# A two-block transformer kernel on one core: feature tiles cast one by one as the last projection tile frees them, and weight panels split ahead of the root

## The reference

```
h = rmsnorm(x, gain)                    # x * rsqrt(mean(x*x) + eps) * gain
x = x + mixer(h) @ w_out                # 1024 x 1024: "mix", "pw2", "mix2" in the kernel
h = rmsnorm(x, gain)
x = x + (silu(h @ w_gate) * (h @ w_up)) @ w_down    # 2816 hidden: "up1/dn1", "up2/dn2", "up3/dn3"
```

## Time and profile before

| | us |
|---|---|
| median of 3 runs | 1957.59 |
| lowest and highest run | 1955.42, 1958.98 |
| the profiled execution, its own time | 1949.41 |
| its span, first to last instruction | 1947.6 |
| PE busy | 1857.5 (95%) |
| DVE busy | 1068.3 (55%) |
| ACT busy | 712.2 (37%) |
| POOL busy | 206.7 (11%) |
| mean granted clock of PE | 0.969 |

### The profile page before, as it was taken

The page is one execution under the profiler, slowest core; times in us unless marked ns, Lnnn a source line. Parts: engine busy times, 40 slices in busy tenths (PEclk is TensorE's granted clock), DMA queues, the critical chain, the costliest instruction groups (busy, mean ns, idle before and its releaser), DMA issues.

```text
span 1947.6 us, 22792 instructions
## 1 busy us (share of the span) xinstructions
PE 1857.5 (95%) x8596; PEld 1532.3 (79%) x8596; DVE 1068.3 (55%) x1304; ACT 712.2 (37%) x799; POOL 206.7 (11%) x125
## 2 busy tenths in 40 slices
PE   7899999999999999699999999899999999999997
PEld 5788877888888788477888888678888788888876
DVE  6647654444444678755444433556845544444455
ACT  4326544434333311245343423432223544332343
POOL 1600000000000476300000000011720000000000
PEclk9889999999999999899999999898999999999999
DMA  5310123333233311032333233222113233323332
GB/s 164 102 49 1 44 65 108 87 107 86 81 104 96 87 51 58 22 87 67 106 86 108 73 99 94 81 86 67 53 59 87 76 97 86 108 77 111 89 89 77
DMA packets 280027, 159.49 MB, mean 82 GB/s; under 512 B 7776, under 2 KB 278016, under 8 KB 279968
## 3 DMA queue, kind: packets, MB, share of 16 engines
q1 hardware_dynamic: 278912, 155.44, 27.8%
q0 software_dynamic: 624, 1.67, 0.3%
q10 hardware_dynamic: 432, 1.57, 0.2%
HBM read 156.56 MB, written 2.10 MB: 81 GB/s over the span
## 4 chain that ended last, share of the span: by engine, by line
PE 89%; DVE 7%; ACT 2%; issue 1%; DMA 0%; POOL 0%; DVEq 0%; SPq 0%; ACTq 0%
PE ps L744 28%; PE ps L746 27%; PE ps L745 27%; PE ps L919 2%; PE ps L904 1%; DVE wlo L1182 1%; PE ps L881 1%; PE ps L1075 1%; DVE rstd L1224 1%; DVE sqacc L1202 1%; DVE ps L1568 1%; DMA raw<-in_nsa_w_in_dram 0%; ACT act_hi L481 0%; DVE act_lo L1212 0%; PE ps L1102 0%
## 5 line engine op out<-in xcount | busy, mean ns | idle before, releaser
L744 PE MATMUL ps<-act_hi,whi 128*128 128x512 f32 x1764 | 704.1, 399 | 44.8 <-DVE act_lo L1214 28.9
L745 PE MATMUL ps<-act_lo,whi 128*128 128x512 f32 x1764 | 696.2, 395 | 0.0
L746 PE MATMUL ps<-act_hi,wlo 128*128 128x512 f32 x1764 | 695.8, 394 | 0.0
L1182 DVE TENSOR_TENSOR wlo<-raw,whi 128x2048 fp32r<-128x2048 f32 (+1 forms) x157 | 359.9, 2293 | 231.2 <-ACT whi L472 230.1
L744 PEld LDWEIGHTS ps<-act_hi,whi 128*128 128x128 f32 x1764 | 336.6, 191 | 130.7 <-issue 37.0
L746 PEld LDWEIGHTS ps<-act_hi,wlo 128*128 128x128 f32 x1764 | 336.7, 191 | 71.9
L745 PEld LDWEIGHTS ps<-act_lo,whi 128*128 128x128 f32 x1764 | 337.0, 191 | 69.7 <-issue 1.2
L472 ACT ACTIVATE whi<-raw 128x2048 fp32r<-128x2048 f32 (+1 forms) x165 | 310.4, 1881 | 212.1 <-PE ps L746 211.6
L1196 DVE TENSOR_TENSOR t<-ps,rstd 128x512 f32<-128x512 f32 (+1 forms) x151 | 103.5, 687 | 229.5 <-PE ps L746 229.3
L744 PE MATMUL ps<-hid_hi,whi 128*128 128x512 f32 x528 | 208.1, 394 | 0.0
L746 PE MATMUL ps<-hid_hi,wlo 128*128 128x512 f32 x528 | 207.0, 392 | 0.0
(11 more groups left out here) (297 smaller groups left out, 1565.6 us busy)
## 6 DMA issues: line engine op xcount, KB each, us to landing
raw<-in_ffn_w_gate_dram SPq DMA_DIRECT2D x44, 512.0 KB, 3.9
raw<-in_ffn_w_up_dram SPq DMA_DIRECT2D x44, 512.0 KB, 5.1
raw<-in_w_gate_upffn_dram SPq DMA_DIRECT2D x44, 512.0 KB, 4.5
raw<-in_ffn_w_down_dram SPq DMA_DIRECT2D x32, 384.0 KB, 3.7
raw<-in_conv_w_pw_dram SPq DMA_DIRECT2D x24, 512.0 KB, 4.3
raw<-in_w_in_dram SPq DMA_DIRECT2D x24, 512.0 KB, 4.4
raw<-in_ffn_w_down_dram SPq DMA_DIRECT2D x32, 320.0 KB, 4.1
raw<-in_nsa_w_in_dram SPq DMA_DIRECT2D x14, 512.0 KB, 4.7
```

What stands on the lines that cost most here:

```text
L744: pe.matmul(out, lhs[0], rhs[0], start=start, stop=False)
L745: pe.matmul(out, lhs[0], rhs[1], start=False, stop=False)
L746: return pe.matmul(out, lhs[1], rhs[0], start=False, stop=stop)
L1182: ve.tensor_tensor(wlo[:, n % 2, a], raw[:, n % 2, a], whi[:, n % 2, a].bitcast(F32), ALU.subtract)\
```

## The change

Four things are rearranged; no arithmetic is added or left out.

1. `late` on ACT and DVE. The last output tile of a projection is the last reader of the activations. PE now raises `act_free` after each of its first seven feature tiles, and ACT casts the next part's `act_hi[k]` as each is released; DVE makes the low parts of tiles 0 to 5 ahead of taking the last output tile into x, and those of 6 and 7 behind it, ahead of the last addition of squares.
2. `first_panel` on PE. The first panel of "up1", "up2", "up3" and "pw1" runs by feature tiles, both output tiles for each, and the sum of squares stands before feature tile 5.
3. The split of the feed-forward's second panel (panel 1) stands ahead of root and reciprocal; in the loop each split moves to the end of the step before. The last two hidden tiles are written out behind the loop.
4. `last_panel` on PE, and the one-pass PE loop around a projection's last two panels is written out.

```
             def late(q, name, use):
                 for i in range(4):
                     hi(N0[name] + i + 1)
                     for k in (2 * i, 2 * i + 1):
+                        if k == KD - 1:
+                            for kk in range(KD - 1):
+                                act.wait_ge(sem("act_free"), 7 * use + kk + 1)
+                                cast(act_hi[:, kk], x[:, kk], f"xhi{q}", gain(q, kk))
                         act.wait_ge(bank_free, T0[name] + k + 5)
+                        if k == KD - 1:
+                            act.wait_ge(panel_done, N0[name] + 4)
+                            cast(act_hi[:, k], x[:, k], f"xhi{q}", gain(q, k))
                         square(q, k, x[:, k])
-                act.wait_ge(panel_done, N0[name] + 4)
-                for k in range(KD):
-                    cast(act_hi[:, k], x[:, k], f"xhi{q}", gain(q, k))
...
             def ffn(f, q, up_, dn, qn):
+                hi(N0[up_] + 1)
                 root(q)
...
+            def first_panel(name, act_wait, mid=None):
+                n, T = N0[name], T0[name]
+                pe.wait_ge(split_done, n + 1)
+                pe.wait_ge(bank_free, T + 2)
+                for k in range(KD):
+                    if mid and k == 5:
+                        mid()
+                    pe.wait_ge(sem(act_wait), k + 1)
+                    for c in range(2):
+                        ins = mm3(bank(T + c)[:, :], slot(n, k, 256, c * P), act_k(k), k == 0, k == KD - 1)
+                        if k == KD - 1:
+                            ins.then_inc(panel_done if c else tile_done, 1)
+
+            def last_panel(name):
+                n, T = N0[name] + 3, T0[name] + 6
+                pe.wait_ge(split_done, n + 1)
+                tile(T, 0, lambda k: slot(n, k), act_k, range(KD), tile_done)
+                pe.wait_ge(bank_free, T + 2)
+                for k in range(KD):
+                    mm3(bank(T + 1)[:, :], slot(n, k, 256, P), act_k(k), k == 0, k == KD - 1)\
+                        .then_inc(sem("act_free") if k < KD - 1 else panel_done, 1)
...
-                panel2(up_, 0, act_wait=f"act{q}", after=lambda: sumsq(q))
+                first_panel(up_, f"act{q}", lambda: sumsq(q))
                 panel2(up_, 1)
...
-            panel2("pw1", 0, act_wait=f"act{CONVIN}", after=lambda: sumsq(CONVIN))
+            first_panel("pw1", f"act{CONVIN}", lambda: sumsq(CONVIN))
...
 (DVE, late)
+                        if k == KD - 1:
+                            low_norm(q, k - 1)
+                            low_norm(q, k)
                         add_square(q, k)
-                for k in range(KD):
-                    low_norm(q, k)
+                        if k == KD - 2:
+                            for kk in range(KD - 2):
+                                low_norm(q, kk)
...
             def ffn(f, q, up_, dn, qn):
+                lo(N0[up_] + 1)
                 inv(q)
```

More of the change, by code:

```diff
@@ L597, in late, with hidden @@
                     for k in (2 * i, 2 * i + 1):
+                        if k == KD - 1:
+                            for kk in range(KD - 1):
+                                act.wait_ge(sem("act_free"), 7 * use + kk + 1)
+                                cast(act_hi[:, kk], x[:, kk], f"xhi{q}", gain(q, kk))
                         act.wait_ge(bank_free, T0[name] + k + 5)
+                        if k == KD - 1:
+                            act.wait_ge(panel_done, N0[name] + 4)
+                            cast(act_hi[:, k], x[:, k], f"xhi{q}", gain(q, k))
                         square(q, k, x[:, k])
[L600 to L604 removed]
+            late(FFN1, "mix", 0)
             def ffn(f, q, up_, dn, qn):
+                hi(N0[up_] + 1)
                 root(q)
[L608 to L614 removed]
+                def hidden(i, j, more):
+                    act.wait_ge(bank_free, 4 * i + (T0[up_] + 2 * j + 5))
+                    act.activation(t3[:, j], t1[:, j], ACT.Silu).then_inc(sem("silu_ready"), 1)
+                    act.wait_ge(sem("hidden_set"), 2 * i + (KF * f + j + 1))
+                    cast(hid_hi[:, bass.ds(2 * i + j, 1), :], t1[:, j], "hidden_hi")
+                    if more:
+                        hi(N0[up_] + j + 2, i)
+                with act.Fori(0, KF // 2 - 1) as i:
+                    for j in range(2):
+                        hidden(i, j, True)
+                hidden(KF // 2 - 1, 0, True)
+                hidden(KF // 2 - 1, 1, False)
                 with act.Fori(0, 2) as i:
@@ L649, in _ @@
                 cast(act_hi[:, k], t3[:, k % 2], "zhi")
-            late(FFN2, "pw2")
+            late(FFN2, "pw2", 1)
             ffn(1, FFN2, "up2", "dn2", FINAL)
@@ L712, in _ @@
                 cast(act_hi[:, h], t1[:, h % 2], "go_hi")
-            late(FFN3, "mix2")
+            late(FFN3, "mix2", 2)
             ffn(2, FFN3, "up3", "dn3", PLE)
@@ L962, in _ @@
             panel2("mix", 1)
-            with pe.Fori(1, 2) as i:
-                for j in range(2):
-                    panel2("mix", j, i)
+            panel2("mix", 0, 1)
+            last_panel("mix")
             def ffn(f, q, up_, dn):
-                panel2(up_, 0, act_wait=f"act{q}", after=lambda: sumsq(q))
+                first_panel(up_, f"act{q}", lambda: sumsq(q))
                 panel2(up_, 1)
@@ L1012, in _ @@
             panel2("pw2", 1)
-            with pe.Fori(1, 2) as i:
-                for j in range(2):
-                    panel2("pw2", j, i)
+            panel2("pw2", 0, 1)
+            last_panel("pw2")
             ffn(1, FFN2, "up2", "dn2")
@@ L1148, in _ @@
             panel2("mix2", 1)
-            with pe.Fori(1, 2) as i:
-                for j in range(2):
-                    panel2("mix2", j, i)
+            panel2("mix2", 0, 1)
+            last_panel("mix2")
             ffn(2, FFN3, "up3", "dn3")
@@ L1498, in _, with hidden @@
             late(FFN1, "mix")
             def ffn(f, q, up_, dn, qn):
+                lo(N0[up_] + 1)
                 inv(q)
-                with ve.Fori(0, KF // 2) as i:
-                    for j in range(2):
[L1504 to L1513, removed]
+                def hidden(i, j, more):
+                    scaled(t1[:, j], first(up_, j, i))
+                    scaled(t2[:, j], second(up_, j, i))
+                    ve.wait_ge(sem("silu_ready"), 2 * i + (KF * f + j + 1))
+                    ve.wait_ge(bank_free, 4 * i + (T0[up_] + 2 * j + 6))
+                    ve.tensor_tensor(t1[:, j], t2[:, j], t3[:, j], ALU.mult).then_inc(sem("hidden_set"), 1)
+                    k = bass.ds(2 * i + j, 1)
+                    ve.wait_ge(sem("hidden_hi"), 2 * i + (KF * f + j + 1))
+                    ve.tensor_tensor(hid_lo[:, k, :], t1[:, j], hid_hi[:, k, :].bitcast(F32), ALU.subtract)\
+                        .then_inc(sem("hidden_lo"), 1)
+                    if more:
+                        lo(N0[up_] + j + 2, i)
@@ L1514, in ffn @@
+                with ve.Fori(0, KF // 2 - 1) as i:
+                    for j in range(2):
+                        hidden(i, j, True)
+                hidden(KF // 2 - 1, 0, True)
+                hidden(KF // 2 - 1, 1, False)
                 if qn == FINAL:
```

2 lines of the change are left out of this document (1 added, 1 removed).

## The result

| | before | change |
|---|---|---|
| median of the runs beside each other | 1956.51 (4 runs) | 1934.7 (4 runs) |
| lowest and highest run | 1955.12, 1958.98 | 1927.9, 1939.3 |
| ratio, 95% interval | | 0.9884, 0.9847 to 0.9921 |
| the profiled execution: its time, its span | 1949.41, 1947.6 | 1927.9, 1926.1 |
| mean granted clock in it | 0.969 | 0.975 |

The change is faster by 21.8 us; 17.1 was forecast. The forecast of 1940.5 lies above all four runs. Their median is at the low edge of the range (1934.5 to 1947.5), and the ratio forecast, 1940.5 / 1957.59 = 0.9913, is inside the interval. So there are two things to explain: the 17 us that were argued, and why the first four runs showed more.

A forecast was written before the change was run, and what follows sets the result against it. TensorE bounds the kernel with 89% of the span, so only holes can be won: 18.46 us at three handovers less 1.36 at "pw1" is 17.10; 1949.41 becomes 1932.3, plus 8.2 gives 1940.5 us, range 1934.5 to 1947.5.

The forecast's parts named there:

- the sum of 49 steps and 0.90: Each handover, projection's last matmul to panel 1: 49 matmuls of 0.2265 us plus sum of squares 0.90, 12.00 us.
- The spare time before panel 2: Split of panel 2 ready at 295.4, wanted by PE at 298.6: 3.2 us to spare.
- the second rival: Handovers: casts don't run ahead, first hole and slow clock stay, 4.2 us won, 1953.4 us; chance 0.05.
- the hole: PE's wait before panel 1 of "pw1" grows from 2.04 to 3.4 us; 1.36 us counted as lost.
- The clock behind the hole: Stretch after the "pw1" hole: whether the clock falls again is worth at most 1.7 us either way.
- Increments and banks: 21 increments in the projections' last tiles: taken as nothing, bound 0.7 us; bank changes every three matmuls: no slowing counted.
- 8.2 above it: Whole program: median of runs shown exceeds the profiled execution by 8.2 us; same difference added to 1932.3, giving 1940.5.
- its own bounds of 1935 to 1945: Forecast's bounds from clock after "pw1" hole (1.7), increments (0.7) and the 8.2 us profile-to-runs difference; forecast's chance 0.82.
- The sum of 17.10: Whole program: 18.46 us won at three handovers less 1.36 lost at "pw1", 17.10 us less.
- the first panels keep their pace: Denies the rival that bank changes every three matmuls slow four first panels: up to 43.5 us more, 1984; chance 0.03.
- The returning wait: Before panel 2 at three handovers: root's chain over 3.2 us late, PE stands, at worst 5.5 us, 1946.0; chance 0.10.

## Why the prediction was right or wrong

**The place and the mechanism: right.** Three handovers of 12.01 us where the sum of 49 steps and 0.90 gave 12.00. The gains, 6.63 + 6.72 + 5.08 = 18.43, were forecast as 18.46. Counted from the projection's last matmul (275.15 here, 275.68 there, so 0.53 comes off each forecast time), the chain also came out term by term: casts done 275.78 (forecast 275.9), six low parts 276.20 (276.4), the eighth 278.35 (278.6), sum of squares 282.18 (282.2), split of panel 1 282.21 (282.8), reciprocal 287.79 (287.8), split of panel 2 295.10 (294.9).

**The spare time before panel 2: right**, 2.8 to 2.9 us against 3.2; in the run with the late sum the wait came back once that was used up.

**Which part pays.** The sum has the gain of the three handovers as a whole; the second rival priced the wait for the split at 3 x 1.84 = 5.5 us of it. The runs agree: 12.9 us for the casts ahead, the other 5.5 for the split ahead of the root, nothing for the order by feature tiles.

**"pw1": the hole right, what follows it mis-sized.** 3.38 us stand where 3.4 was forecast, and 1.34 of the 1.36 arrive at panel 1. The clock behind the hole was said to be worth at most 1.7 either way. It was 0 in one execution, so the loss was 1.36, and 1.6 in two (166.82 - 163.85 = 2.97, and 3.06). The bound held against the profiled execution before. But that one had a fall of its own there: in the runs with the casts alone and with the splits alone, whose "pw1" is as before, none came, and its next 74 matmuls took 17.10 us against 18.68.

**Increments and banks: nothing, as taken.** The Trainium skill, "TensorE: Matmul & The Clock Gate", section "The cost: per-tile semaphore tail", gives some 26 ns for each increment of matmuls packed as tiles into the array; carried over to these 454 that is an estimated 12 us. The run shows 0.00. The Trainium skill, same page, section "A second HAM failure mode: psum-queue depth-cycling", would have the clock swing when matmuls cycle through banks; the window with a bank change every three matmuls has granted clock 1.00. Neither rule shows in this kernel, where PE doesn't wait at these points.

**The step that failed: "The median of the runs shown is 1957.59, 8.2 above it; I carry the same difference over"**, and its own bounds of 1935 to 1945. That term took the difference between one execution and the median of three for a constant of the kernel, and gave it bounds from a spread of 3.6 us. The runs show that it only says where these executions stood in a wider spread: 13.4 us in 37 later runs of the kernel before. How long PE runs at 1.2 GHz in stretches that the change doesn't touch varies from execution to execution. In the linear attention alone it is 3.4, 13.7, 17.1 or 20.5 us over the thirteen profiles here, at 0.46 us for each us; the profile of the change is the only one with 3.4, and the profile before has 13.7. The three runs that the forecast started from were at the upper end, some 3 us above the later medians, and the change's four were two and two. From a base of 1954.6 the same sum gives 1937.5, and the two samples of the change measured 1936.82 and 1938.36. So the first median gave 21.8, outside the forecast's own 1935 to 1945, and the two samples of five and six runs 0.0094 x 1955 = 18.4 and 18.0. That it still fell inside the range, by 0.2 us, is luck. The sum of 17.10 stands within 1.3 us of these; over the touched stretches the traces show 15.4, 15.5 and 17.1. The Trainium skill, same page, section "What's actually happening", says of the slow matmuls at a kernel's start that their number varies between runs of one kernel; the traces show the like in its middle, of which that section says nothing: 157.79 and 165.67 us of the same instructions.

What starts such a fall in one execution and not in another, as in the third handover of the kernel with the splits alone, was not settled, and no run tried to force it. Nor does the mean clock settle a run's time: at 0.966 the runs of before took from 1953.96 to 1959.95 us.

**The rivals.** The casts do run ahead; no wait came back; the first panels keep their pace. The returning wait comes when the sum of squares is 4.08 us later, not in the change.

## What to carry to other kernels

When a product hands over to the next, ask of each preparing step what it really waits for: here the casts needed each feature tile's last reader and not the end of the projection, and the weight split needed nothing from the root that stood ahead of it. Price a hole together with the slower clock behind it, and then look at every place that shares the code: "pw1" had the same root ahead of its split, was left as it was, and cost 4.8 to 6.5 us more than need be. For a gain of 1% compare stretches between the same instructions of two traces, and take a median only from enough runs, when the runs lie in two groups 8 us apart.

## What the hardware showed that was not expected

- The 15 runs of the change fall in groups by the mean granted clock: 0.972 to 0.975 at 1927.9 to 1930.9 us, 0.967 to 0.969 at 1936.8 to 1939.3. The time goes in the linear attention and in the attention (over the thirteen profiles, 117.8 to 121.4 us between the same matmuls there, with 0 to 10.2 us at 1.2 GHz).
- The hole of 2.93 us before the first panel of "up3" was followed by 3.4 us at 1.2 GHz in the kernel with the splits alone and by none in the kernel before; in the kernel before, the holes ahead of "up1" and "up2" were followed by 3.4 us each.
- Increments between matmuls cost nothing: 454 of them in 349.81 us, +0.00.
- A PSUM bank change after every three matmuls cost nothing over 349.81 us (+0.00).
